# Attention jobs of 128 queries with one softmax unit per head, in a hybrid attention and RWKV-7 layer

## The reference

```
def prompt_attention(q_lat, q_rope, ckv, krope):
    k_chunk = jnp.arange(T) // CHUNK                        # CHUNK = 64
    def one_block(i):
        q_chunk = (q0 + jnp.arange(Q_BLOCK)) // CHUNK
        mask = k_chunk[None, :] <= q_chunk[:, None]
        return mla_attend(ql, qr, ckv, krope, mask)         # softmax(scores) times values
...
def wkv_scan(S0, r, decay, k, v, kk, a):
    def step(S, inp):
        sa = jnp.einsum('bhvk,bhk->bhv', S, -kk_t)
        S = (S * w_t[:, :, None, :] + sa[..., None] * (kk_t * a_t)[:, :, None, :]
             + v_t[..., None] * k_t[:, :, None, :])
        return S, jnp.einsum('bhvk,bhk->bhv', S, r_t)
```

## Time and profile before

| | |
|---|---|
| runs of the kernel | 1932.43, 1935.83, 1938.1 us; median 1935.83 |
| span of the profiled execution | 1930.4 us (no other time of that execution is recorded) |
| TensorE busy | 1816.3 us (94%), 17762 products |
| VectorE, ScalarE, GpSimd busy | 989.9, 629.2, 349.6 us |
| stage with scan and attention | 345 to 967 us from the start |

### The profile page before, as it was taken

One profiled execution on the slowest core, in us unless ns is written; L12 is line 12 of the kernel. 1 busy time (PEld: TensorE's weight loads), 2 busy tenths in 40 slices (PEclk: granted clock), 3 DMA queues, 4 the chain that ended last, 5 costly groups with the idle time before them and its releaser, 6 DMA issues. The chain is left out here.

```text
span 1930.4 us, 41344 instructions
## 1 busy us (share of the span) xinstructions
PE 1816.3 (94%) x17762; PEld 1533.5 (79%) x17762; DVE 989.9 (51%) x1526; ACT 629.2 (33%) x1262; POOL 349.6 (18%) x411
## 2 busy tenths in 40 slices
PE   5999999988998998998899989999999999999996
PEld 3988889566576576666644689999999999999994
DVE  4697765745554654565527643333333333333347
ACT  4744433444444444444423432112112112112114
POOL 0032220235534434444500010000000000000002
PEclk9999999999999998999999999999999999999998
DMA  9367774210110110103132121011011011011122
GB/s 343 122 173 195 186 194 150 64 38 27 51 41 27 51 41 27 51 27 87 53 123 85 63 97 55 23 55 55 22 55 55 23 55 55 22 55 55 44 93 93
DMA packets 126323, 151.19 MB, mean 78 GB/s; under 512 B 83168, under 2 KB 98144, under 8 KB 125824
## 3 DMA queue, kind: packets, MB, share of 16 engines
q1 hardware_dynamic: 126144, 148.56, 24.0%
HBM read 118.05 MB, written 30.50 MB: 77 GB/s over the span
## 5 line engine op out<-in xcount | busy, mean ns | idle before, releaser
L429 PE MATMUL ps<-fhi,whi 128*128 128x364 f32 (+1 forms) x1056 | 349.0, 330 | 7.8 <-DVE wlo L421 5.7
L429 PE MATMUL ps<-flo,whi 128*128 128x364 f32 (+1 forms) x1056 | 346.8, 328 | 0.0
L429 PE MATMUL ps<-fhi,wlo 128*128 128x364 f32 (+1 forms) x1056 | 345.8, 327 | 0.0
L421 DVE TENSOR_TENSOR wlo<-wraw,whi 128x1024 fp32r<-128x1024 f32 x70 | 86.9, 1243 | 244.4 <-ACT whi L417 244.4
L429 PEld LDWEIGHTS ps<-fhi,whi 128*128 128x128 f32 x1056 | 198.5, 188 | 9.5 <-issue 4.4
L429 PEld LDWEIGHTS ps<-fhi,wlo 128*128 128x128 f32 x1056 | 199.2, 189 | 0.0
L429 PEld LDWEIGHTS ps<-flo,whi 128*128 128x128 f32 x1056 | 198.5, 188 | 0.2
L1895 DVE TENSOR_TENSOR acc<-acc,ps 128x364 f32<-128x364 f32 (+1 forms) x240 | 126.6, 531 | 100.8 <-PE ps L2424 100.5
L841 POOL TENSOR_TENSOR nlev<-gm,con 64x256 f32<-64x256 f32 x204 | 152.8, 749 | 114.2 <-DVE gm L1623 100.1
L429 PE MATMUL ps<-hhi,whi 128*128 128x364 f32 (+1 forms) x464 | 161.3, 348 | 1.5 <-DVE hlo L1491 1.2
L2424 PE MATMUL ps<-ahi,dhi 128*128 128x364 f32 (+1 forms) x480 | 158.5, 330 | 2.4 <-DVE acc L1895 2.4
(11 more groups left out here) (249 smaller groups left out, 3357.7 us busy)
## 6 DMA issues: line engine op xcount, KB each, us to landing
wraw<-in_w_tiles SPq DMA_DIRECT2D x68, 512.0 KB, 4.1
late<-in_ada_t SPq DMA_DIRECT2D x32, 512.0 KB, 3.5
ci<-scan SPq DMA_DIRECT2D x17, 768.0 KB, 4.5
draw<-in_w_down SPq DMA_DIRECT2D x20, 512.0 KB, 3.3
slab<-in_ada_w SPq DMA_DIRECT2D x4, 2048.0 KB, 18.0
x<-in_x_t SPq DMA_DIRECT2D x4, 1456.0 KB, 9.6
bg<-bg SPq DMA_DIRECT2D x17, 256.0 KB, 2.8
x<-x_mid SPq DMA_DIRECT2D x1, 4352.0 KB, 12.8
```

The lines of the kernel that those rows point to most:

```text
L421: nc.vector.tensor_tensor(wlo[u][:, :, :], wraw[u][:, :, :], whi[u][:, :, :].bitcast(F32), ALU.subtract).then_inc(w_lo, 1)
L429: mm = nc.tensor.matmul(ps[:, 3 * u + c, 0:n], w[u][:, k, :], x[:, k, :], start=(k == 0 and i == 0), stop=(k == KD - 1 and i == 2))
```

## The change

Prompt jobs have 128 queries, so there are 8. Each has two score units, one per head, with 128 queries on 128 partitions and 128(job + 1) keys. The first 64 queries of a job must not see its last 64 keys: a product of a row of ones with a row of -1e30 (one partition deep, 64 by 64) is accumulated onto that corner of the scores. A turn of a prompt job has at most 2 tiles, each with one transpose per head; `values` multiplies 128 probability columns instead of 64. The sample job comes first in each pair, with turns of up to 4 tiles. A pair has 20 score units as before, 25 turns for 30, and 3 output blocks for 6. The probabilities of every second prompt job lie in the sample job's buffer.

```
-PROMPT_JOBS = list(reversed(range(TP // C)))
-SAMPLE_JOB, SAMPLE_PARTS, SAMPLE_AT = TP // C, 4, 6
+PROMPT_JOBS = list(reversed(range(TP // P)))
+SAMPLE_JOB, SAMPLE_PARTS = TP // P, 4
-JOB_ORDER = PROMPT_JOBS[:SAMPLE_AT] + [SAMPLE_JOB] + PROMPT_JOBS[SAMPLE_AT:]
+JOB_ORDER = [SAMPLE_JOB] + PROMPT_JOBS
...
-    n, most = (job // 2 + 1, 4) if job < SAMPLE_JOB else (1 + PAST // P, 3)
+    n, most = (job + 1, 2) if job < SAMPLE_JOB else (1 + PAST // P, 4)
...
-OUT_BLOCKS = [JOB_ORDER[0:3], JOB_ORDER[3:6], [SAMPLE_JOB], JOB_ORDER[7:11], JOB_ORDER[11:15], JOB_ORDER[15:17]]
+OUT_BLOCKS = [JOB_ORDER[0:3], JOB_ORDER[3:7], JOB_ORDER[7:9]]
...
-    units += scores(2) + [("norm", JOB_ORDER[0], 0)] + [("value", g, 0) for g in range(1, len(V_GROUPS))]
+    units += scores(2) + [("value", 1, 0)]
+    units += scores(2) + [("norm", SAMPLE_JOB, 0)] + [("value", g, 0) for g in range(2, 4)]
+    units += scores(2) + [("value", g, 0) for g in range(4, len(V_GROUPS))]
...
-                exps = [] if job == SAMPLE_JOB else scores(2 if i < SAMPLE_PARTS else 1)
+                exps = scores(2)
...
+                    step.done(nc.vector.reciprocal(sm[:, RECIP + u:RECIP + u + 2], sm[:, SUM + u:SUM + u + 2]))
+                    for e in range(2):
+                        keys = probs_of(job, e)[:, 0:P * (job + 1)]
+                        nc.vector.tensor_scalar(keys, keys, sm[:, RECIP + u + e:RECIP + u + e + 1], None, ALU.mult).then_inc(p_norm, 1)
...
+                        mm = nc.tensor.matmul(ps[:, bank, 0:n], qt[part][0:96, P * job:P * job + P], kt[part][0:96, k0:k0 + n],
+                                              start=True, stop=True, skip_group_check=True)
+                if job != SAMPLE_JOB:
+                    mm = nc.tensor.matmul(ps[0:C, bank, n - C:n], con[0:1, K_ONES:K_ONES + C], con[0:1, K_CS:K_CS + C], start=False, stop=True,
+                                          skip_group_check=True)
...
+                        for e in range(2):
+                            at = P * (2 * (t - t0) + e)
+                            mm = nc.tensor.transpose(ps[:, 4, at:at + P], probs_of(job, e)[:, k0:k0 + P], ident)
...
+                        r, p0 = slice(64 * e, 64 * e + 64), 2 * cols * (t - t0) + cols * e
+                        mm = nc.tensor.matmul(ps[r, 5, c0:c0 + cols], vt[0:rows, at, r], pt[0:rows, slot, p0:p0 + cols], start=(t == 0), stop=(t == n - 1))
...
+    t[0, K_CS:K_CS + C] = NEG
```

More of the change, by code:

```diff
@@ L1261, in exponentials @@
                 else:
[L1262 to L1265, removed]
+                    at, u = JOB_ORDER.index(job), stat_of(job, part)
+                    act.wait_ge(t_mm, N_TURNS * hp + (T_END[JOB_ORDER[at - 2]] if at >= 2 else 0) + 1)
+                    dst, stats = probs_of(job, part)[:, 0:P * (job + 1)], (NMAX + u, SUM + u)
                 nc.scalar.activation(dst, score_cols(x), ACT.Exp, bias=sm[:, stats[0]:stats[0] + 1],
@@ L1274, in put_out @@
                 block, low = OUT_AT[job]
-                a, n = C * low, C * len(OUT_BLOCKS[block])
+                a, n = job_cols(low)[0], sum(job_cols(x)[1] for x in OUT_BLOCKS[block])
                 act.wait_ge(o_mm, N_TURNS * hp + T_END[job] + 1)
@@ L1743, in job_norm @@
                 else:
[L1744 to L1747, removed]
+                    u = stat_of(job, 0)
+                    step.done(nc.vector.reciprocal(sm[:, RECIP + u:RECIP + u + 2], sm[:, SUM + u:SUM + u + 2]))
+                    for e in range(2):
+                        keys = probs_of(job, e)[:, 0:P * (job + 1)]
+                        nc.vector.tensor_scalar(keys, keys, sm[:, RECIP + u + e:RECIP + u + e + 1], None, ALU.mult).then_inc(p_norm, 1)
             def put_keys(l, hp):
@@ L2248, in scores @@
             def scores(x, hp):
-                job, _ = SCORES[x]
-                q0 = TP if job == SAMPLE_JOB else C * job
+                job, part = SCORES[x]
                 if x >= 2:
@@ L2261, in scores @@
                     pe.wait_ge(qd_ev, 6 * hp + 6 + 1)
+                if x == SAMPLE_PARTS:
+                    pe.wait_ge(angles_in, 16)
                 before_small()
                 for b, k0, n in score_pieces(x):
-                    for e in range(2):
-                        mm = nc.tensor.matmul(ps[64 * e:64 * e + 64, 2 * (x % 2) + b, 0:n], qt[e][0:96, q0:q0 + C], kt[e][0:96, k0:k0 + n],
-                                              start=True, stop=True)
+                    bank = 2 * (x % 2) + b
+                    if job == SAMPLE_JOB:
+                        for e in range(2):
+                            mm = nc.tensor.matmul(ps[64 * e:64 * e + 64, bank, 0:n], qt[e][0:96, TP:T], kt[e][0:96, k0:k0 + n], start=True, stop=True)
+                    else:
+                        mm = nc.tensor.matmul(ps[:, bank, 0:n], qt[part][0:96, P * job:P * job + P], kt[part][0:96, k0:k0 + n],
[3 more added lines that the diff above has]
+                                          skip_group_check=True)
                 mm.then_inc(s_mm, 1)
@@ L2278, in turn @@
                     _, k0, rows = tile_rows(job, t)
-                    mm = nc.tensor.transpose(ps[0:rows, 4, P * (t - t0):P * (t - t0) + P], probs_of(job)[:, k0:k0 + rows], ident)
+                    if job == SAMPLE_JOB:
+                        mm = nc.tensor.transpose(ps[0:rows, 4, P * (t - t0):P * (t - t0) + P], spr[:, k0:k0 + rows], ident)
+                    else:
+                        for e in range(2):
+                            at = P * (2 * (t - t0) + e)
+                            mm = nc.tensor.transpose(ps[:, 4, at:at + P], probs_of(job, e)[:, k0:k0 + P], ident)
                 mm.then_inc(t_mm, 1)
@@ L2289, in values @@
                 before_small()
+                (c0, cols), slot = job_cols(job), (N_TURNS * hp + x) % RING
+                c0 -= job_cols(low)[0]
                 for t in range(t0, t1):
```

38 lines of the change are left out of this document (21 added, 17 removed).

## The result

| | before | after |
|---|---|---|
| median, runs on the same chip | 1935.38 us (4 runs) | 1956.25 us (4 runs, 1952.64 to 1961.2) |
| ratio after to before | | 1.0117, 95% interval 1.009 to 1.0144 |
| span of the profiled execution | 1930.4 us | 1950.9 us |

The change makes the kernel 1.2% slower. The forecast was slower, 1943 us; the result lies 13 us above it, at the upper end of its range (1923 to 1957).

A forecast was written before the change was run, and what follows sets the result against it. TensorE was taken to bound the stage from 345 to 967 us, as the sum of its work and waits. 7.0 (work) + 5.1 - 2 - 5.8 + 5 - 2 = +7.3 us gave a median of 1943 us, range 1923 to 1957.

The forecast's parts named there:

- (b): 64 mask products on TensorE, each two records and a change of shape, taken at 0.18 us: +11.5 us.
- (a): Prompt scores on TensorE: not halved, 2048 more columns in four pairs at 1.7 ns: +3.5 us.
- (f): Clock in the stage: about 12 us lost before, 10.2 after, from three waits each bringing 7 us at half clock: -2 us.
- dear masks: Rival, "Dear masks and late copies": masks at 0.29 us (+7) and exponentials in full (+5): 1955 us, chance 0.12.
- (c): `values` on TensorE: 144 records of 128 columns for 288 in a pair, and twenty turns fewer: -5.6 us.
- (e): Start of each pair: scan waits behind the sample's division, 15.0 us for 9.9: +5.1 us.
- (g): Output blocks: waits of `values` for the copy of the block before fall from 8 to 2.2 us: -5.8 us.
- (h): Two exponentials of a job in a row on ScalarE delay the scan's copies: +5 us (0 to +10).
- (i): The other waits, some 40 us: larger last units, so small jobs cover the scan's steps more: -2 us (-8 to +6).
- fewer instructions: Rival: TensorE bound by giving out instructions, so dropped records bring more than their columns, 20 us less: 1923 us, chance 0.06.
- better cover: Rival: waits ahead of `level_x` and `level_t` fall by 11 us and clock loss by 5 more: 1927 us, chance 0.26.
- everything cancels: Rival: masks at their lower bound of 0.06 us (-7.5): 1936 us, chance 0.18.

The follow-up runs named there:

- e2: The changed kernel with every mask product issued twice, same result: 1956.46 us, ratio 1.0123 to the kernel before.
- e9: The changed kernel with the mask as a product of full shape, 128 rows deep and 128 columns wide: 1945.46 us, ratio 1.0061 to the kernel before.
- e10: The changed kernel with the mask 64 rows deep and 64 columns wide, like the scan's small products: 1951.33 us, ratio 1.0094 to the kernel before.
- e6: The kernel before with 4 output blocks per pair instead of 6, nothing else: 1932.16 us, ratio 0.999.
- e5: The changed kernel with the sample job's division two value groups and two score units later: 1943.73 us, ratio 1.0051 to the kernel before.
- e11: e4 with VectorE zeroing the 64 probabilities behind each job's first half, so every `values` product can take 128 columns: 1935.98 us, ratio 1.0018.
- e8: e11 with the later division of e5: 1919.4 us, ratio 0.9928 to the kernel before.
- e3: The changed kernel with the mask one row deep but 128 columns wide in its stationary operand: 1960.57 us, ratio 1.0135 to the kernel before.
- e4: The changed kernel with score units of 64 queries, both heads side by side, no mask, last `values` key tile as four small products: 1937.89 us, ratio 1.002.

## Why the prediction was right or wrong

The sign was right, and so was the account of what bounds the stage: TensorE does, scores do not halve, and the masks outweigh what `values` and transposes give. The size was not: the sum was 7.3 us and the spans show 20.5. What failed is the price of the masks in (b), with one change of the array's form in place of two and products at half their cost, and the same change in (a), which left it out (together +8.9 us). The sign of the clock in (f) failed too (+5.4). By its steps:

- **(a) Scores, +3.5.** Measured +7.5 with the sample's. About 3.4 of it are the columns as forecast: a unit grows by 1.67 ns a column in the trace, for 1.7. What was left out is the entry: a unit of 128 queries behind 64-wide products leads on 0.21 us later than its columns ask, where a unit 64 wide ahead of its like took 0.05.
- **(b) Masks, +11.5: the step that failed.** Measured 16.4 us by their line and 18.4 by leaving them out, 0.29 us each for 0.18. It was priced as "the two records and 0.12 for the change". The two records were read at 0.06 us from the earlier trace rows, where 16 records of the scan's y run two column halves side by side; a mask has nothing beside it and costs 0.12 (e2). And the change was counted once, where it is about 0.10 us each time and lies on both sides of a mask in full-width surroundings (e9, e10): 0.40 us there, 0.25 elsewhere. The rival "dear masks" had this price, and 0.29 as its point.
- **(c) Values, -5.6.** Measured -6.0.
- **(d) Transposes, -2.4.** Measured -4.0.
- **(f) Clock, -2: wrong in sign.** 34.1 us at half clock for 27.3, +3.4 us of work (the value projection, which lies in the three stretches behind the start waits, shows +3.7). Behind the three start waits came 3.4 us each and not 7, as the windows show; but three stretches of 6.8 us came behind waits of about 2 us in the later jobs, and one of 3.4 behind a wait of 1.84, which the step did not look for. It had also read the old loss as 12 us from a rounded 0.98, where half of 27.3 is 13.7.
- **(e), (g), (h), (i), the waits.** Forecast 5.1 - 5.8 + 5 - 2 = +2.3; measured +2.4. (e) The start waits are 3.41, 3.63, 3.63 and, at 854 us in the last pair, 0.58 us for a forecast of 4.5, 4.6, 4.6 and 1.3: +1.4 for +5.1. The chain in the second pair took 5.7 us from the end of the sample scores (547.73) to the end of the copy of y (553.47), for 6.5, and TensorE had 2.2 us of its own work beside it, for 1.95. (g) 8.0 became 2.4 us, as forecast. e6 shows that 2.2 us of this are the number of blocks; by difference the rest comes with the sample job's new place, where its block change of 1.50 us a pair is gone. (h) and (i) together, by difference, +6.6 for +3; the run of two exponentials does stop TensorE, 1.84 us at 443 us, behind ScalarE's copies. That the waits' sum came out right is luck: (e) was 3.7 too high and these two as much too low.

The terms that missed are (a) + 4.0, (b) + 4.9 by its line and (f) + 5.4, less 2.0 from (c) and (d): 12.3 of the 13.2 us. (The (a) and (b) split follows the table; leaving the masks out moves 2 us from one to the other.)

Of the rivals, "fewer instructions" is refuted by (c): the 576 dropped records of `values` brought what their columns and turns are worth. "Better cover" is refuted by the idle time at `level_x` and `level_t`, which rose from 32.8 to 37.2 us in place of falling by 11, and "everything cancels" by the masks. "Dear masks" came within 1 us of the time (1955), in part by luck: it holds the forecast's -2 for the clock. The Trainium skill ("TensorEngine Tiling (Array Packing)", Key Properties) says that a change of tiling mode drains the engine. The runs agree in that each change costs time, and give the size here: about 0.10 us.

The price of the division's place was underrated in another way. The forecast gave it 5.1 us of waits and a gain of clock; undoing it brought 12.5 us in the changed kernel (e5) and, by the ratios, 0.9% or 17 us in the best version (e11 to e8). Half of the second is clock, but only about 2 us of the first. Why the same edit freed the clock in e8 and hardly in e5 stays open.

## What to carry to other kernels

Price a product that is put between others by its form, not by its size: masks of different form but the same result cost between 0.51 (e3) and 0.01 us (e10), by their own form and by their neighbours', and the one with 256 times the arithmetic was cheaper than the thin one. Take the price of one instruction only from rows in which it runs alone as it will, not from a group in which two halves of the array share the time. And compare the mean granted clock of all runs before a gain is put down to an edit: about half of e8's gain was clock. Where TensorE is the bound but has a tenth of waits, work taken away can return as waiting (e11) until the wait that comes last at that place is taken away with it (e8).

## What the runs showed of the hardware that was not expected

- A mask 64 deep and 64 wide ahead of the scan's products of the same form is all but free (products behind it start 0.01 us later), though it comes before them in the queue; ahead of full-width work the same product costs 0.25 us.
- In the changed kernel the clock fell for 3.4 us behind waits of 3.4 to 3.6 us, and for 6.8 behind some of 1.9 to 2.1 us. In e11 one of the waits of 3.63 us brought 6.8. The length at half clock did not follow the length of the wait, so a forecast per wait is not to be had from these traces. What the runs do show is that of two kernels with the same products, the one with the start waits (e11) had 30.7 us at half clock and the other (e8) 13.7.
- Two products 64 columns wide, side by side, take as long for a column as one of 128: ahead of work 64 wide, a unit leads on after 0.91 us for 512 keys (the kernel before) and 1.34 for 768 (e4), so it grows by 1.68 ns for a column of both heads, and a unit of 128 queries by 1.67. So a wider product brought nothing here.
